# Query weights: ScalarE converts pieces 5, 6 and 7 ahead of the copies of query products 2, 3 and 4

## The chip, the cores and the metric

The kernel runs on one core of a Trainium2 chip. The metric is the device time of one execution in microseconds (us). Before the change, three executions took 1545.81, 1546.57 and 1550.71 us; the median is 1546.57 us.

## The reference, cut to what matters

The program computes three transformer layers over 256 tokens of width 1024, in float32. The change lies in the first layer's feed-forward part, which picks experts by product keys:

```python
def peer_ffn(xn, w_query, subkeys, u_tab, v_tab):
    q = (xt @ w_query).reshape(T, PEER_HEADS, 2, PEER_QDIM // 2)     # 256 tokens, 8 heads x 256
    s = jnp.einsum('thpd,hpkd->thpk', q, subkeys).astype(jnp.float32)
    sv, si = lax.top_k(s, PEER_TOPK)
    # 16 x 16 sums of both halves, top 16 of them: expert ids and softmax gates
    ug = u_tab[ec]
    vg = v_tab[ec]
    act = jax.nn.gelu(jnp.einsum('thkd,td->thk', ug, xc))
    return jnp.einsum('thk,thkd->td', (gc * act), vg)
```

For each of 256 tokens and 8 heads, 16 experts are chosen, and of each of these two rows of 1024 floats are fetched from tables in HBM.

## The kernel before, in words

**Weights in two parts.** Each weight piece (1 MB, 128 x 2048 float32) is loaded by SyncE into a raw buffer. It is then split: ScalarE writes a rounded copy, the high part (`split_hi`, its operation is at line 432), and VectorE or GpSimd subtracts it from the raw data, which gives the low part (`split_lo`, line 439). TensorE multiplies with three passes (high by high, low by high, high by low; lines 2048 to 2050). The high and low parts live in four slots, 0 to 3. `split_hi` waits until the piece that held the slot before has been used by TensorE.

**Query pieces.** The query weights are 8 pieces, one for each head. Pieces 0 to 3 lie in slots 0 to 3, pieces 4 and 6 in slot 2, and pieces 5 and 7 in slot 3. So the high part of piece 4 waits for query product 2, piece 5 for product 3, piece 6 for product 4, and piece 7 for product 5. Query product m is 48 matmuls (`queries(m)`) into one PSUM bank. TensorE's order is: product 1, product 2, the scores of the first heads (`scores(0)`), products 3 to 7, `scores(1)` to `scores(7)` (line 2308), and then the sums of expert rows (line 2332).

**Evacuation in a fixed order.** The semaphore `evac_done` counts the banks that have been emptied, and each copy waits until all earlier jobs were emptied. The order of jobs around the change is written in `PLAN`: query product 2, then the score job of `scores(0)`, then query products 3 to 7, then the other score jobs. ScalarE copies the query products (`query_cols(m)`, line 918). VectorE copies the result of `scores(0)` (line 1660), and it waits for `evac_done` to have counted query product 2.

**VectorE's order** around the change is written out by hand. It does the low part of piece 3, the copy of `scores(0)`, the low parts of pieces 4 and 5, four dot products with expert rows (line 1629), the low parts of pieces 6 and 7, the routing of the second unit, and more dot products:

```python
split_lo(v, "query", 3)
v.wait_ge(evac_done, J["score"])
freed(nc.vector.tensor_copy(SCORE[:, 2 * P:BANK], bank(j)[:, 2 * P:]), j, wait=True)
for n in range(4, 6):
    split_lo(v, "query", n)
```

**Expert rows.** A unit is one head for one half of the tokens, and there are 16 of them. GpSimd issues 16 gathers of 1 MB for each unit (line 627). Their buffers overlay the query weights: gather 6 of the first unit waits for the low part of piece 6, gather 7 for that of piece 7, gathers 9 and 11 for the use of pieces 6 and 7 by TensorE, and gather 13 for all scores. Later units' gathers wait until TensorE has summed the rows that were in the buffers.

Of the kernel before, what the change touches and what calls it, by code (L numbers as in the profile page):

```python
# [80 lines left out]
def query_job(m):  # L81

    return J[f"query_{m}"] if m < 3 else J["query_rest"] + m - 3
# [57 lines left out]
def build(nc, a, out, at):  # L141
    ctx = ExitStack()
    with ctx:
# [44 lines left out]
        PHI = place("ple_hi", [P, 2, S], O_B + 1024, F32R)  # L188
        PLO = place("ple_lo", [P, 2, S], O_B + 1536, F32R)
        C = sb("consts", [P, sum(n for _, n in at.values())])  # L190
        VEC = sb("vec_cols", [P, 72])
        CONV = sb("conv_cols", [P, 2, 4 * 2 * FT])
# [233 lines left out]
        def split_hi(eng, copy, name, n):  # L426

            w = pieces[name, n]
            eng.wait_ge(raw_loaded[w.r], w.landed)
            if w.before is not None:  # L430
                eng.wait_ge(*pieces[w.before].used)
            copy(w.hi[:, :], w.raw[:, :]).then_inc(hi_ready[w.h], 1)  # L432
# [286 lines left out]
        def _(act):  # L719
# [76 lines left out]
            def split(name, n):  # L796
                split_hi(act, act.copy, name, n)
# [112 lines left out]
            def query_cols(m):  # L910
                j = query_job(m)
                act.wait_ge(pe_done, j + 1)
                act.wait_ge(evac_done, j)
                if m == 0:
                    d, src = qT[:, 0:2, P:S], PS[:, j % 8, 2 * P:4 * P]
                else:
                    d, src = qT[:, 2 * m:2 * m + 2, :], PS[:, j % 8, :]
                act.copy(d, src.rearrange("p (c t) -> p c t", c=2)).then_inc(evac_done, 1)
# [6 lines left out]
            def weights(u, q, b):  # L925
                act.wait_ge(sem("dots_done"), u * 4 + (b + 1))
                nc.scalar.activation(r_act[:, b % 2], r_dot[:, b % 2], ACT.Gelu).then_inc(sem("gelu_done"), 1)  # L927
                if b == 0:
                    act.wait_ge(sem("gates_ready"), u + 1)
                act.wait_ge(sem("gelu_done"), u * 4 + (b + 1))  # L930
                for k in range(4):
                    ins = nc.scalar.activation(r_wt[:, b % 2, k:k + 1], r_act[:, b % 2, k:k + 1], ACT.Copy,
                                               scale=r_gate[:, q, 4 * b + k:4 * b + k + 1])
                ins.then_inc(sem("weights_ready"), 1)
# [17 lines left out]
            gate_exp(0)  # L952
            query_cols(1)
            query_cols(0)
            for n in range(4, 8):
                split("query", n)
                query_cols(n - 2)
            weights(0, 0, 0)
            diag(0, 0, wait=False)
            query_cols(6)  # L960
# [225 lines left out]
        def _(v):  # L1186
# [532 lines left out]
            def relative(n):  # L1719

                L, bt, e, _, _ = level(n)
                ref = bt[:, :, L - 1:L].broadcast_to([P, 4 * S // (2 * L), 2 * L])
                step(nc.vector.tensor_tensor(e, bt, ref, ALU.subtract), "h_rel")

            def operands(n):

                L, _, e, qv, kv = level(n)
                if n < 3:
                    v.wait_ge(sem("h_relexp"), 2 * n + 2)
                else:  # L1730
                    v.wait_ge(evac_done, END[f"hg_R{n}"])
                step(nc.vector.tensor_tensor(e[:, :, L:2 * L], e[:, :, L:2 * L], qv[:, :, L:2 * L], ALU.mult), "h_lev", False)
                step(nc.vector.tensor_tensor(e[:, :, 0:L], e[:, :, 0:L], kv[:, :, 0:L], ALU.mult), "h_lev")
# [924 lines left out]
```

## Time and profile before

| quantity | value |
|---|---|
| median of three executions | 1546.57 us |
| profiled execution, own time | 1549.39 us |
| its span on the core | 1547.6 us |
| TensorE busy | 1380.5 us (89%) |
| VectorE busy | 1034.6 us (67%) |
| ScalarE busy | 710.4 us (46%) |
| GpSimd busy | 572.9 us (37%) |
| query products 2 to 7 and scores, in the span | from 170.36 us to about 211.7 us |

Busy time is summed over the whole span, while the stages have different limits. In the rows, PE is TensorE's matmul, PEld its weight load, DVE is VectorE, ACT ScalarE, POOL GpSimd and SP SyncE. `L432` is line 432. A bracket such as `[4.70 <-ACT work_a L918]` says how long the engine was idle just before and what ended that.

### The profile page before, as it was taken

The page shows a single profiled execution, that of the slowest core. Times are in us where ns is not written, and L with a number is a line of the kernel's source. Part 1 is how long each engine was busy: PE and PEld are TensorE (multiplying, and loading weights), DVE is VectorE, ACT ScalarE, POOL GpSimd, SP SyncE. Part 2 cuts the span into 40 slices and gives each one's busy share as a digit, 9 for nine tenths or more (in the row PEclk, how much of TensorE's full clock was granted, in tenths as well). Part 3 has the DMA queues.
Part 4 walks back from the last instruction along what each step waited for, and adds up shares of the span by engine and source line. Part 5 has one row for each costly group of instructions (what it writes and reads, how often), then busy time and mean ns, then how long its engine had stood idle before and what let it go on. Part 6 is the DMA issues. An engine that isn't in the chain of part 4 may idle for free.

```text
span 1547.6 us, 18196 instructions
## 1 busy us (share of the span) xinstructions
PE 1380.5 (89%) x5969; PEld 966.9 (62%) x5969; DVE 1034.6 (67%) x1920; ACT 710.4 (46%) x1377; POOL 572.9 (37%) x537
## 2 busy tenths in 40 slices
PE   7989998778777867877778999999999999999998
PEld 6877973333323323333335879788888778888887
DVE  4896777666666766666655548569863586498733
ACT  5535553223333333223324463477654745776534
POOL 2330454333333333333332421045443612364414
PEclk9999999999999999998998999899999999999999
DMA  9286689999999999999997510557665433476650
GB/s 313 88 144 224 245 353 423 420 422 421 422 421 422 421 422 421 423 421 423 421 420 295 191 33 28 164 163 213 194 215 175 160 140 108 121 207 195 216 192 28
DMA packets 180739, 414.99 MB, mean 268 GB/s; under 512 B 9178, under 2 KB 113218, under 8 KB 148418
## 3 DMA queue, kind: packets, MB, share of 16 engines
q0 software_dynamic: 37440, 268.45, 41.8%
q1 hardware_dynamic: 143090, 145.66, 30.6%
q8 instruction: 38, 0.62, 0.2%
q14 instruction: 27, 0.22, 0.0%
q10 hardware_dynamic: 144, 0.04, 0.0%
HBM read 409.93 MB, written 4.19 MB: 268 GB/s over the span
## 4 chain that ended last, share of the span: by engine, by line
PE 53%; DMA 23%; DVE 9%; ACT 6%; POOL 5%; issue 4%; ACTq 0%; POOLq 0%; DVEq 0%
DMA expert_rows<-in_peer_uv,route_idx 16%; PE ps L2332 10%; PE ps L2501 10%; PE ps L2048 8%; PE ps L2049 8%; PE ps L2050 8%; PE ps L2502 5%; DMA work_b<-in_peer_uv,route_idx 5%; POOL expert_rows L627 2%; DVE weights_lo L439 2%; DMA work_b<-in_peer_u,route_idx 1%; ACT weights_hi L432 1%; POOL weights_lo L587 1%; PE ps L2013 1%; POOL ple_proj_lo L587 1%
## 5 line engine op out<-in xcount | busy, mean ns | idle before, releaser
L1629 DVE CUSTOM_DVE_ANT_0 expert_rows<-expert_rows,ps 128x1024 f32<-128x1024 f32 x180 | 219.4, 1220 | 134.4 <-DMA expert_rows<-in_peer_uv,route_idx 131.5
L2332 PE MATMUL ps<-expert_rows,proj 128*128 128x512 f32 x512 | 244.1, 633 | 65.9 <-ACT proj L941 59.3
L587 POOL TENSOR_TENSOR weights_lo<-weights_raw,weights_hi 128x512 fp32r<-128x512 f32 x120 | 159.7, 1366 | 381.7 <-ACT weights_hi L432 308.5
L627 POOL DMA_INDIRECT expert_rows<-in_peer_uv,route_idx x191 | 184.3, 965 | 285.9 <-PE ps L2332 216.0
L432 ACT CAST weights_hi<-weights_raw 128x2048 fp32r<-128x2048 f32 x98 | 185.4, 1917 | 101.8 <-PE ps L2050 81.6
L2332 PEld LDWEIGHTS ps<-expert_rows,proj 128*128 128x128 f32 x512 | 100.9, 202 | 208.2 <-issue 127.5
L2501 PE MATMUL ps<-x_normT,weights_hi 128*128 128x512 f32 x640 | 222.5, 394 | 0.0
L439 DVE TENSOR_TENSOR weights_lo<-weights_raw,weights_hi 128x2048 fp32r<-128x2048 f32 x68 | 160.6, 2370 | 64.1 <-ACT weights_hi L432 63.7
L927 ACT ACTIVATE proj<-proj 128x4 f32<-128x4 f32 x64 | 13.1, 205 | 411.7 <-DVE proj L1629 404.6
L2048 PE MATMUL ps<-weights_hi,x_normT 128*128 128x512 f32 (+1 forms) x496 | 189.6, 382 | 12.7 <-DVE weights_lo L439 7.4
L2049 PE MATMUL ps<-weights_lo,x_normT 128*128 128x512 f32 (+1 forms) x496 | 185.8, 375 | 0.0
L2050 PE MATMUL ps<-weights_hi,x_normT 128*128 128x512 f32 (+1 forms) x496 | 185.7, 374 | 0.0
L2502 PE MATMUL ps<-x_normT,weights_lo 128*128 128x256 f32 x640 | 177.3, 277 | 0.0
L2332 PE MATMUL ps<-expert_rows,scratch 128*128 128x512 f32 x252 | 121.7, 630 | 28.2 <-ACT scratch L941 28.2
L2501 PEld LDWEIGHTS ps<-x_normT,weights_hi 128*128 128x128 f32 x640 | 120.0, 188 | 27.9
L2502 PEld LDWEIGHTS ps<-x_normT,weights_lo 128*128 128x128 f32 x640 | 120.2, 188 | 0.0
L2048 PEld LDWEIGHTS ps<-weights_hi,x_normT 128*128 128x128 f32 x496 | 94.2, 190 | 34.6 <-issue 8.0
L2332 PEld LDWEIGHTS ps<-expert_rows,scratch 128*128 128x128 f32 x252 | 49.8, 202 | 99.0 <-issue 59.5
L2050 PEld LDWEIGHTS ps<-weights_hi,x_normT 128*128 128x128 f32 x496 | 94.1, 190 | 16.9
L2049 PEld LDWEIGHTS ps<-weights_lo,x_normT 128*128 128x128 f32 x496 | 94.3, 190 | 15.8 <-issue 0.2
L1860 DVE SCALAR_TENSOR_TENSOR work_a<-ps,conv_cols,work_a 128x254 f32<-128x254 f32 (+1 forms) x176 | 76.4, 475 | 29.3 <-ACT work_a L1076 25.2
L694 POOL TENSOR_TENSOR hidden_hi<-work_a 128x256 f32 (+1 forms) x44 | 41.9, 951 | 100.3 <-ACT work_a L1056 100.0
(367 smaller groups left out, 2413.2 us busy)
## 6 DMA issues: line engine op xcount, KB each, us to landing
weights_raw<-in_ffn_up SPq DMA_DIRECT2D x88, 512.0 KB, 5.1
weights_raw<-in_ffn_down SPq DMA_DIRECT2D x22, 1024.0 KB, 4.9
weights_raw<-in_ab_w_in SPq DMA_DIRECT2D x14, 1024.0 KB, 5.2
weights_raw<-in_w_in SPq DMA_DIRECT2D x12, 1024.0 KB, 7.9
weights_raw<-in_ple_gate SPq DMA_DIRECT2D x8, 1024.0 KB, 6.6
weights_raw<-in_c_w_in SPq DMA_DIRECT2D x6, 1024.0 KB, 5.9
weights_raw<-in_w_out SPq DMA_DIRECT2D x4, 1024.0 KB, 12.4
weights_raw<-in_peer_w_query SPq DMA_DIRECT2D x4, 1024.0 KB, 12.2
```

Of the source, the lines that this page charges most:

```text
L432: copy(w.hi[:, :], w.raw[:, :]).then_inc(hi_ready[w.h], 1)
L439: eng.tensor_tensor(w.lo[:, :], w.raw[:, :], w.hi[:, :].bitcast(F32), ALU.subtract).then_inc(lo_ready[w.h], 1)
L587: ins = pool.tensor_tensor(w.lo[:, c], w.raw[:, c], w.hi[:, c].bitcast(F32), ALU.subtract)
L627: nc.gpsimd.indirect_dma_start(out=dst, out_offset=None, in_=table, in_offset=bass.IndirectOffsetOnAxis(ap=r_idx[:, q, n:n + 1], axis=0)). ...
L1629: ins = nc.vector.tensor_tensor_reduce(out=rows, in0=rows, in1=tokens, scale=1.0, scalar=0.0, op0=ALU.mult, op1=ALU.add, accum_out=r_dot[: ...
L1860: ins = nc.vector.scalar_tensor_tensor(out=d, in0=PS[:, (j0 + 2 * q + g) % 8, 0:S - n], scalar=CONV[:, l, bass.ds(i * RING + (tap * 2 * FT ...
L2048: pe.matmul(o, x[0], w[0], start=first, stop=False)
L2049: pe.matmul(o, x[0], w[1], start=False, stop=False)
L2050: return pe.matmul(o, x[1], w[0], start=False, stop=last)
L2332: ins = pe.matmul(PS[:, (J[f"peer_{t}"] + m) % 8, :], DIAG[b][:, k, :], rows[:, m * BANK:(m + 1) * BANK], start=False, stop=False, skip_gr ...
L2501: pe.matmul(b.rearrange("p (a t) -> p a t", a=2), hi[:, c, g, :], x_both(c), start=c == 0, stop=False)
L2502: ins = pe.matmul(b[:, 0:S], lo[:, c, g, :], XHI[:, c, :], start=False, stop=c == KC - 1)
```

## The change

ScalarE's order in the query stage is changed. Before, it converted piece n and then copied product n - 2, for n from 4 to 7. After it, piece 4 is converted first, then pieces 5, 6 and 7 are each converted ahead of the copy of products 2, 3 and 4, and the copy of product 5 follows at the end. The same instructions are issued, with the same waits.

```diff
             gate_exp(0)
             query_cols(1)
             query_cols(0)
-            for n in range(4, 8):
+            split("query", 4)
+            for n in range(5, 8):
                 split("query", n)
-                query_cols(n - 2)
+                query_cols(n - 3)
+            query_cols(5)
             weights(0, 0, 0)
             diag(0, 0, wait=False)
             query_cols(6)
```

| ScalarE's order | before | after |
|---|---|---|
| 1 | convert 4 | convert 4 |
| 2 | copy 2 | convert 5 |
| 3 | convert 5 | copy 2 |
| 4 | copy 3 | convert 6 |
| 5 | convert 6 | copy 3 |
| 6 | copy 4 | convert 7 |
| 7 | convert 7 | copy 4 |
| 8 | copy 5 | copy 5 |

## Rows read from the trace of the kernel before

**Rows 1.** The page: DMA share and GB/s in 40 slices; the last chain's shares.

```profile
DMA  9286689999999999999997510557665433476650
GB/s 313 88 144 224 245 353 423 420 422 421 422 421 422 421 422 421 423 421 423 421 420 295 191 33 28 164 163 213 194 215 175 160 140 108 121 207 195 216 192 28
DMA expert_rows<-in_peer_uv,route_idx 16%; PE ps L2332 10%; PE ps L2501 10%; PE ps L2048 8%; PE ps L2049 8%; PE ps L2050 8%; PE ps L2502 5%; DMA work_b<-in_peer_uv,route_idx 5%; POOL expert_rows L627 2%; DVE weights_lo L439 2%; DMA work_b<-in_peer_u,route_idx 1%; ACT weights_hi L432 1%; POOL weights_lo L587 1%; PE ps L2013 1%; POOL ple_proj_lo L587 1%
```

**Rows 2.** Windows, 190 to 210: length, each engine's busy time, PEclk, DMA share, GB/s.

```profile
190.00:195.00 5.00, 5.00 (x44) 5.00 (x44) 3.73 (x5) 1.63 (x3) 0.50 (x1) 1.00 0.60 249
195.00:200.00 5.00, 5.00 (x44) 5.00 (x43) 3.76 (x10) 4.85 (x12) 1.21 (x2) 1.00 0.62 213
200.00:205.00 5.00, 5.00 (x44) 5.00 (x43) 4.72 (x22) 2.30 (x5) 3.01 (x4) 1.00 0.80 287
205.00:210.00 5.00, 5.00 (x46) 5.00 (x46) 4.90 (x10) 2.93 (x5) 2.89 (x2) 1.00 1.01 395
```

**Rows 3.** Chain of waits, 140 to 420: start, length, what.

```profile
205.60 6.25 PE ps L2308 x56
...
256.51 19.62 DMA expert_rows<-in_peer_uv,route_idx
```

**Rows 4.** Timeline of ScalarE: start, length, instruction, idle before.

```profile
176.45 1.91 ACT L432 CAST weights_hi<-proj 128x2048 fp32r<-128x2048 f32 x1 [4.98 <-PE ps L2050]
178.26 0.58 ACT L918 COPY work_a<-ps 128x512 f32<-128x512 f32 x1
182.65 1.90 ACT L432 CAST weights_hi<-scratch 128x2048 fp32r<-128x2048 f32 x1 [3.81 <-PE ps L2050]
184.46 0.58 ACT L918 COPY work_a<-ps 128x512 f32<-128x512 f32 x1
188.41 1.91 ACT L432 CAST weights_hi<-expert_rows 128x2048 fp32r<-128x2048 f32 x1 [3.38 <-PE ps L2050]
...
194.17 1.90 ACT L432 CAST weights_hi<-expert_rows 128x2048 fp32r<-128x2048 f32 x1 [3.37 <-PE ps L2050]
```

**Rows 5.** Timeline of VectorE.

```profile
151.99 2.29 DVE L439 TENSOR_TENSOR weights_lo<-weights_raw,weights_hi 128x2048 fp32r<-128x2048 f32 x1 [0.65 <-ACT weights_hi L432]
...
178.87 0.42 DVE L1660 COPY proj<-ps 128x256 f32<-128x256 f32 x1 [4.70 <-ACT work_a L918]
179.32 2.29 DVE L439 TENSOR_TENSOR weights_lo<-proj,weights_hi 128x2048 fp32r<-128x2048 f32 x1
184.65 2.29 DVE L439 TENSOR_TENSOR weights_lo<-scratch,weights_hi 128x2048 fp32r<-128x2048 f32 x1 [3.04 <-ACT weights_hi L432]
...
191.44 2.28 DVE L439 TENSOR_TENSOR weights_lo<-expert_rows,weights_hi 128x2048 fp32r<-128x2048 f32 x1
196.17 2.29 DVE L439 TENSOR_TENSOR weights_lo<-expert_rows,weights_hi 128x2048 fp32r<-128x2048 f32 x1 [2.44 <-ACT weights_hi L432]
```

**Rows 6.** Timeline of TensorE: the first matmuls of a product after a wait, and of products 3 and 4.

```profile
154.34 0.38 PE L2048 MATMUL ps<-weights_hi,x_normT 128*128 128x256 f32 x1
...
176.56 0.36 PE L2048 MATMUL ps<-x_normT,weights_hi 128*128 128x256 f32 x1
...
182.39 0.28 PE L2048 MATMUL ps<-x_normT,weights_hi 128*128 128x256 f32 x1
```

**Rows 7.** Timeline of GpSimd: gathers 6 and 7 of the first unit.

```profile
194.50 0.94 POOL L627 DMA_INDIRECT expert_rows<-in_peer_uv,route_idx  x1 [14.55 <-DVE weights_lo L439]
199.24 0.94 POOL L627 DMA_INDIRECT expert_rows<-in_peer_uv,route_idx  x1 [3.79 <-DVE weights_lo L439]
```

**Rows 8.** TensorE after its two longest later idles: timeline rows.

```profile
831.65 0.77 PE L2048 MATMUL ps<-weights_hi,x_normT 128*128 128x512 f32 x1 [2.74 <-DVE weights_lo L439]
...
839.65 1.97 PE L2013 MATMUL ps<-consts,x_res 128*128 128x128 f32 x8 [3.65 <-DVE x_res L1308]
```

**Rows 9.** Windows of one us after those two restarts.

```profile
834.00:835.00 1.00, 1.00 (x5) 0.83 (x4) 0.96 (x2) 0.00 (x0) 0.00 (x0) 0.70 1.06 406
...
844.00:845.00 1.00, 1.00 (x4) 0.81 (x3) 0.40 (x2) 0.91 (x5) 0.00 (x0) 0.57 0.02 8
```

## The prediction

> **What bounds the kernel now.** I began with the page's slices and its chain. The reader sees a long middle stretch in which the DMA engines are saturated at about 421 GB/s, which are the gathers of expert rows, and a chain that spends 16% of the span on those gathers [rows 1]. The question is what decides when that stretch begins. The windows around it answer: between 190 and 205 us the DMA engines are busy for 0.60, 0.62 and 0.80 of the time, and only from 205 us on for all of it, while TensorE is busy for the whole of each 5 us [rows 2]. The chain of waits says the same: it runs through TensorE up to the scores (56 matmuls at 205.60 us) and first passes through a gather at 256.51 us [rows 3]. So in the query stage TensorE sets the time, and the gathers behind it are started by what TensorE and the splitting of weights release.
>
> Then I read the three engines' timelines side by side. TensorE goes straight from product 3 (176.56) into product 4 (182.39): 5.83 us for one product, no idle time [rows 6]. ScalarE waits for TensorE ahead of every conversion: 4.98, 3.81, 3.38 and 3.37 us, and always on the product whose slot it overwrites [rows 4]. VectorE waits 4.70 us for the copy of product 2 before it may copy the scores (178.87), and only behind that comes the low part of piece 4, from 179.32 to 181.61 [rows 5]. TensorE needs that low part at 182.39. Its cover is 182.39 - 181.61 = 0.78 us, and that is all the slack there is.
>
> **The change part by part.** Nothing is added or removed: no instruction, no DMA, no semaphore. Five copies and conversions trade places, and what matters is which waits they now stand behind.
>
> *Conversions 5, 6 and 7 earlier by one copy: gain nothing.* Each starts when its product has ended. Conversion 5 starts at 182.65, 0.26 us after product 4 started, and ScalarE had been idle for 3.81 us before it [rows 4]. The copy that stood ahead of it was long done. From below the gain is 0, and from above it is at most one copy, 0.58 us, if a conversion had ever waited for one; the idle times exclude that, so I take 0.
>
> *Copy of product 2, behind conversion 5: this is the cost.* Conversion 5 waits for product 3, which TensorE ends at about 182.4 in either kernel. The conversion then runs from 182.65 and the copy behind it starts at 184.46, as the copy of product 3 did, and ends at 184.46 + 0.58 = 185.04 [rows 4]. VectorE's copy of the scores starts 0.03 us after that copy (178.87 against 178.26 + 0.58), so now at 185.07. The low part of piece 4 follows after 0.45 us (179.32 - 178.87), at 185.52, and ends at 185.52 + 2.29 = 187.81 [rows 5]. Handing a low part to TensorE costs 0.06 us (154.34 against 151.99 + 2.29) [rows 5, 6]. Product 4 therefore starts at 187.87 instead of 182.39: TensorE stands still for 5.48 us. The first matmul after a wait holds TensorE for a little longer than one in a row (0.36 to 0.28), which adds 0.08. Term: 5.5 us.
>
> What is queued behind the waiting copy on ScalarE is only conversion 6, and that waits for product 4 anyway. Behind VectorE's waiting copy stand the low parts of pieces 4 and 5; TensorE waits for the first, and the second is done at 187.81 + 2.29 = 190.1, well ahead of product 5 (187.87 + 5.83 = 193.7). SyncE's loads of pieces 6 and 7 wait for product 1 and don't move. GpSimd's queue stays as it is.
>
> *Clock after the stall.* TensorE has nowhere in this stretch stood still for so long; the nearest rows are two restarts after idles of 2.74 and 3.65 us [rows 8]. After the first the granted clock is at the lower level (1.2 GHz of 2.4) until about 834.6: the window 834 to 835 has a mean of 0.70, so 0.6 of it was at half [rows 9]. That is 834.6 - 831.65 = 2.95 us. After the second it is low until 844.86 (mean 0.57: 0.86 at half), 5.2 us. At half clock half of that time is lost: 1.5 and 2.6 us. An idle of 5.5 us is longer than both, so a fall is to be expected; I take the middle, 2.0 us, as an estimate. Its ends are 0 (no fall) and 2.6, and a little more for a longer low stretch, 3.3.
>
> The Trainium skill, page "TensorE: Matmul & The Clock Gate", Part 1, says of modelling that "the ramp penalty is <1% of a typical kernel span" and that one should not fit a count of cold matmuls. By that advice the term would be left out, and the sum would be the stall alone (the first rival below). The two restarts in rows 8 and 9 speak against leaving it out here, where it is a quarter of the effect.
>
> *Is there a second stall?* With the clock's term product 5 starts at 187.87 + 5.83 + 2.0 = 195.7 and product 6 at 201.4. Conversion 6 starts 0.26 after product 5's start, 196.0, ends at 197.9, and its low part is done at 200.2, 1.2 us before product 6. VectorE's four dots (4.5 us, the time between the end of the low part of piece 5, 186.94, and the start of that of piece 6, 191.44) are done by then, at 194.6. Piece 7 goes the same way, 5.7 us later. The copies of products 3, 4 and 5 have nobody waiting for them before the scores at the end. So no second stall: 0.
>
> *What the delay becomes.* Gather 6 was released by the low part of piece 6 (191.44 + 2.28 = 193.72, issued at 194.50) and gather 7 by that of piece 7 (198.46, issued at 199.24) [rows 5, 7]. Both low parts follow TensorE, by about 6.5 and 7.5 us later. Gathers 9, 11 and 13 wait for products 6 and 7 and for the scores. The DMA engines were partly idle between 190 and 205 [rows 2], so there is no stock of issued gathers with which to use the extra time. Their saturated stretch starts about 7.5 us later, and as the same 1 MB gathers then flow at the same rate [rows 1], it ends 7.5 us later. The layers behind it depend on its result, so nothing gives it back.
>
> **Sum.** 5.5 + 2.0 = 7.5 us. Against the profiled execution's own time (span 1547.6, time 1549.39) that is 1556.9. That execution is 2.8 us above the median of the three shown, so against the median it is 1546.57 + 7.5 = 1554.1 us, and that is what I forecast (1.005 of before).
>
> **Rivals.**
>
> *The clock stays up.* The stall alone would be 5.5 us: 1552.1. For it: the rows have only two restarts, with low stretches as different as 2.95 and 5.2 us, so the length is not a constant of the kernel. Against: both were behind idles shorter than this one, and both had a low stretch.
>
> *The gathers swallow the delay (not slower).* If the saturated stretch were limited by a backlog that exists before gather 7, starting TensorE's part 7.5 us later would cost nothing. It decides from the point at which gathers already issued would keep the DMA engines busy until the delayed ones come, some 7 us of work at 200 us. For it: the stretch from 205 us on is DMA-bound. Against: 0.60 and 0.62 busy in the two windows before; the unused 5 x (0.40 + 0.38 + 0.20) = 4.9 us show that there is no backlog there. Price 0: 1546.6; half swallowed gives 1550.3.
>
> *VectorE takes the ready low part ahead of the waiting copy (not slower).* Then the stall vanishes: 1546.6. In the trace the high part of piece 4 was ready at 178.36, VectorE idle, and yet the low part started only behind the copy, at 179.32 [rows 4, 5]. So it goes in order. The Trainium skill, page "Perfetto Trace Analysis", section "Per-engine timelines", calls ScalarE's, VectorE's and GpSimd's execution "strict FIFO"; the trace agrees.
>
> *A second stall at piece 6 or 7.* Their slack is 1.2 us; if a slowed TensorE or a late dot used it up, 1 to 3 us come on top: up to 1557.
>
> **How the numbers follow.** The forecast (stall and a fall of the clock, all of it passed on) gets 0.70, the stall alone 0.10, a second stall 0.05, delay half or wholly swallowed 0.12, in order or other surprises on the fast side 0.03. What a measurement of this kernel can tell from no change is about 0.3%, 4.6 us, so "same" reaches from 1541.9 to 1551.2. The forecast, the stall alone and the second stall lie above that; since executions of before alone spread over 4.9 us, I leave 0.02 of them to "same". Slower 0.83, same 0.14, faster 0.03. The range goes from 1550.3 (half swallowed) to 1557.4 (clock term 3.3 and a small second wait or spread of the executions).
>
> **What would show it right or wrong.** After the change VectorE's line 1660 should wait about 10.9 us instead of 4.7 (it is free from 174.2) and start at 185.1; TensorE should show one idle of about 5.3 us before a matmul of line 2048 at 187.9, released by the low part of line 439, and a granted clock under 1 in the 5 us behind it; gather 7 should be issued at about 206.7 and `scores` begin at about 213. The DMA share in 195 to 205 us should fall well under 0.6. If TensorE has no idle there, the argument is wrong at its root; if it has and the end does not move, the swallowing rival was right.

## The result and the profile after

Twelve executions of the changed kernel have a median of 1554.62 us, twelve of the kernel before 1547.28 us. The ratio is 1.0051 with a 95% interval of 1.0041 to 1.0062: slower by 7.3 us in the medians, 7.9 us by the ratio (6.3 to 9.6 us by its interval). The forecast was 1554.1 us and 1.005.

The profiled execution after has its own time of 1553.87 us (span 1552.1). In the changed file every line behind the edit is two higher: 1660 became 1662, and 2048 to 2050 became 2050 to 2052. The traces also begin at slightly different points: conversion 4 starts at 176.45 before and at 176.55 after, so 0.10 us is to be taken off every shift of the second trace.

ScalarE's timeline after (start, length, instruction, idle before), which answers to [rows 4]:

```profile
176.55 1.91 ACT L432 CAST weights_hi<-proj 128x2048 fp32r<-128x2048 f32 x1 [4.98 <-PE ps L2052]
182.75 1.90 ACT L432 CAST weights_hi<-scratch 128x2048 fp32r<-128x2048 f32 x1 [4.29 <-PE ps L2052]
184.55 0.58 ACT L918 COPY work_a<-ps 128x512 f32<-128x512 f32 x1
196.20 1.91 ACT L432 CAST weights_hi<-expert_rows 128x2048 fp32r<-128x2048 f32 x1 [11.07 <-PE ps L2052]
198.01 0.57 ACT L918 COPY work_a<-ps 128x512 f32<-128x512 f32 x1
201.96 1.91 ACT L432 CAST weights_hi<-expert_rows 128x2048 fp32r<-128x2048 f32 x1 [3.37 <-PE ps L2052]
```

Conversion 5 starts when it did before, since it waits for the same product. The copy of product 2 is now at 184.55 instead of 178.26. VectorE's timeline after, to [rows 5]:

```profile
185.16 0.42 DVE L1662 COPY proj<-ps 128x256 f32<-128x256 f32 x1 [10.90 <-ACT work_a L918]
185.62 2.29 DVE L439 TENSOR_TENSOR weights_lo<-proj,weights_hi 128x2048 fp32r<-128x2048 f32 x1
187.83 2.28 DVE L439 TENSOR_TENSOR weights_lo<-scratch,weights_hi 128x2048 fp32r<-128x2048 f32 x1
...
198.21 2.29 DVE L439 TENSOR_TENSOR weights_lo<-expert_rows,weights_hi 128x2048 fp32r<-128x2048 f32 x1 [3.52 <-ACT weights_hi L432]
203.97 2.29 DVE L439 TENSOR_TENSOR weights_lo<-expert_rows,weights_hi 128x2048 fp32r<-128x2048 f32 x1 [3.47 <-ACT weights_hi L432]
```

The copy of the scores waited 10.90 us instead of 4.70, and the low part of piece 4 ends at 187.91. TensorE's timeline after, to [rows 6], and its granted clock (the column ahead of the last two) in windows of one us:

```profile
187.96 0.58 PE L2050 MATMUL ps<-x_normT,weights_hi 128*128 128x256 f32 x1 [5.31 <-DVE weights_lo L439]
188.34 0.41 PE L2051 MATMUL ps<-x_normT,weights_hi 128*128 128x256 f32 x1
```

```profile
185.00:186.00 1.00, 0.00 (x0) 0.00 (x0) 0.80 (x2) 0.13 (x1) 0.00 (x0) 0.99 1.04 417
186.00:187.00 1.00, 0.00 (x0) 0.00 (x0) 1.00 (x1) 0.00 (x0) 0.00 (x0) 0.50 1.00 418
...
192.00:193.00 1.00, 1.00 (x7) 1.00 (x7) 1.00 (x3) 0.00 (x0) 0.00 (x0) 0.59 0.91 369
193.00:194.00 1.00, 1.00 (x10) 1.00 (x10) 1.00 (x3) 0.00 (x0) 0.00 (x0) 1.00 0.16 66
```

Product 4 starts 5.47 us late (187.96 - 182.39 - 0.10). The clock fell to half during the idle and came back at about 192.8 (the mean of 0.59 means 0.82 us at half): 4.9 us of product 4 ran at half clock. What that cost is seen at the scores. They begin at 213.23 in TensorE's timeline, against 205.43 before: 7.70 us later with the offset taken off, of which 5.47 are the stall and 2.23 the clock and the restart.

GpSimd's gathers 6 and 7, to [rows 7], and the DMA share (the last column but one) in windows of 5 us, to [rows 2]:

```profile
201.28 0.94 POOL L627 DMA_INDIRECT expert_rows<-in_peer_uv,route_idx  x1 [21.24 <-DVE weights_lo L439]
207.04 0.94 POOL L627 DMA_INDIRECT expert_rows<-in_peer_uv,route_idx  x1 [4.82 <-DVE weights_lo L439]
```

```profile
190.00:195.00 5.00, 5.00 (x34) 5.00 (x33) 4.69 (x9) 0.00 (x0) 0.00 (x0) 0.72 0.63 257
195.00:200.00 5.00, 5.00 (x44) 5.00 (x43) 1.79 (x1) 2.39 (x2) 0.00 (x0) 1.00 0.00 0
200.00:205.00 5.00, 5.00 (x44) 5.00 (x43) 1.53 (x2) 2.95 (x3) 0.94 (x1) 1.00 0.40 120
205.00:210.00 5.00, 5.00 (x44) 5.00 (x44) 4.83 (x20) 4.83 (x13) 2.35 (x3) 1.00 0.52 164
```

The DMA engines stand still from 195 to 200 us, where before they were busy for 0.62 of the time. There was nothing to move.

**Where the profiled pair differs from the medians.** The two profiled spans are only 4.5 us apart. Followed through the trace, the shift is still 7.4 us where TensorE waits at 965.65 before and at 973.10 after (7.45 less the offset), and 4.5 at the next such wait, 987.18 and 991.76. Between them the profiled execution of before ran at a lower clock, and the one after did not. The windows of before:

```profile
970.00:975.00 5.00, 5.00 (x24) 3.07 (x22) 3.50 (x4) 1.65 (x3) 0.00 (x0) 0.61 1.05 397
975.00:980.00 5.00, 5.00 (x25) 3.58 (x22) 3.20 (x4) 0.59 (x1) 0.00 (x0) 0.50 1.19 297
980.00:985.00 5.00, 5.00 (x23) 4.28 (x23) 4.82 (x7) 4.49 (x4) 0.00 (x0) 0.86 0.45 113
```

After, the windows from 975 to 990 have 1.00. Of the thirteen traces of this study four show such a fall here, those of before and of runs 1, 4 and 10, with and without the stall in the query stage, so it does not belong to the change. In that pair it masked 2.9 us of the 7.4, and the executions' medians are the better measure.

### The profile page after: what moved, and what is told of

The parts are those of the page before. It is cut to its first block, busy times and chain, and to the rows that moved or that the text cites. A ratio compares the mean times of both kernels' runs of the same rounds, so it can differ in the third digit from the quotient of the medians.

```text
span 1552.1 us, 18196 instructions
## 1 busy us (share of the span) xinstructions
PE 1378.4 (89%) x5969; PEld 965.9 (62%) x5969; DVE 1034.7 (67%) x1920; ACT 710.4 (46%) x1377; POOL 570.3 (37%) x537
## 4 chain that ended last, share of the span: by engine, by line
PE 51%; DMA 23%; DVE 10%; ACT 6%; issue 5%; POOL 5%; ACTq 0%; POOLq 0%; DVEq 0%; SPq 0%
DMA expert_rows<-in_peer_uv,route_idx 15%; PE ps L2503 10%; PE ps L2050 8%; PE ps L2334 8%; PE ps L2052 8%; PE ps L2051 8%; DMA work_b<-in_peer_uv,route_idx 7%; PE ps L2504 5%; DVE weights_lo L439 2%; POOL expert_rows L627 2%; ACT weights_hi L432 2%; POOL weights_lo L587 1%; DMA weights_raw<-in_ab_w_in 1%; PE ps L2015 1%; POOL ple_proj_lo L587 1%
## 5 line engine op out<-in xcount | busy, mean ns | idle before, releaser
L2051 PEld LDWEIGHTS ps<-weights_lo,x_normT 128*128 128x128 f32 x496 | 94.3, 190 | 15.8 <-issue 0.2
```

Source lines behind the costliest of these rows:

```text
L2051: pe.matmul(o, x[0], w[1], start=False, stop=False)
```

## The experiments

A ratio is that of a kernel's time to the time of before, measured beside it, with its 95% interval; 0.1% is 1.55 us. Where starts in two traces are compared with the offset taken off, the offset is again read from conversion 4 (176.45 us in the kernel before).

### 1 and 2: which of the moved copies does it

Experiment 1 moves only the copy of product 2:

```diff
-            for n in range(4, 8):
-                split("query", n)
-                query_cols(n - 2)
+            split("query", 4)
+            split("query", 5)
+            query_cols(2)
+            query_cols(3)
+            for n in range(6, 8):
+                split("query", n)
+                query_cols(n - 2)
```

> Only the copy of query product 2 goes behind conversion 5; conversions 6 and 7 keep their places. Chain theory (copy 2 releases VectorE's copy of the scores, that the low part of piece 4, that TensorE's product 4): the whole effect is here, one TensorE idle of 5.3 us at 182.5 to 187.9, half clock for some 5 us, 7 to 8 us slower than before (ratio 1.005), the same as the full change. Rival (the three earlier conversions share the effect, or the gathers' release): a third of it, 2 to 3 us.

Measured: 1.0037 (1.0024 to 1.0051), 5.7 us, somewhat less than the 7 to 8 us expected. TensorE has the same idle:

```profile
188.55 0.58 PE L2052 MATMUL ps<-x_normT,weights_hi 128*128 128x256 f32 x1 [5.31 <-DVE weights_lo L439]
```

Experiment 2 moves everything else:

```diff
-            for n in range(4, 8):
-                split("query", n)
-                query_cols(n - 2)
+            split("query", 4)
+            query_cols(2)
+            split("query", 5)
+            for n in range(6, 8):
+                split("query", n)
+                query_cols(n - 3)
+            query_cols(5)
```

> Copy 2 keeps its place; only conversions 6 and 7 go ahead of the copies of products 3 and 4. Chain theory: no TensorE idle, no change (ratio 1.000, within 0.15%). Rival (every move costs something): 1.002 to 1.004.

Measured: 1.0000 (0.9989 to 1.0010). There is no wait of TensorE for a low part in this stage. The two together say that the cost sits in the copy of product 2 alone, and that conversions 6 and 7 gain nothing by going first. The ratio of the first is lower than the full change's 1.0051, but the intervals overlap, and the traces agree: with the offsets taken off, the scores begin 7.70 us later than before in run 1 as in the full change, and 0.04 us later in run 2.

### 3: the link through VectorE

The full change, with VectorE's low part of piece 4 ahead of its copy of the scores:

```diff
             split_lo(v, "query", 3)
+            split_lo(v, "query", 4)
             j = J["score"]
             v.wait_ge(evac_done, j)
             freed(nc.vector.tensor_copy(SCORE[:, 2 * P:BANK], bank(j)[:, 2 * P:]), j, wait=True)
-            for n in range(4, 6):
-                split_lo(v, "query", n)
+            split_lo(v, "query", 5)
```

> The full change, and VectorE does the low part of piece 4 ahead of its copy of the first scores, so that this copy no longer stands in front of it. Chain theory: TensorE's idle is gone although copy 2 is as late as in the full change, and the time is that of before (ratio 1.000, within 0.15%). If the order on ScalarE alone did it: 1.005 stays.

Measured: 1.0003 (0.9991 to 1.0014). VectorE's timeline of this kernel, and the one wait that TensorE is left with:

```profile
178.38 2.29 DVE L439 TENSOR_TENSOR weights_lo<-proj,weights_hi 128x2048 fp32r<-128x2048 f32 x1 [4.31 <-ACT weights_hi L432]
184.98 0.42 DVE L1663 COPY proj<-ps 128x256 f32<-128x256 f32 x1 [4.32 <-ACT work_a L918]
185.44 2.29 DVE L439 TENSOR_TENSOR weights_lo<-scratch,weights_hi 128x2048 fp32r<-128x2048 f32 x1
```

```profile
194.57 0.38 PE L2050 MATMUL ps<-x_normT,weights_hi 128*128 128x256 f32 x1 [0.58 <-DVE weights_lo L439]
```

ScalarE's order is that of the full change and the copy of the scores is just as late (184.98), but nothing that TensorE needs at once waits for it, and the loss is gone from the time. The remaining 0.58 us is the low part of piece 6, pushed back because that of piece 5 now stands behind the late copy; the scores begin 0.8 us later than before. So it was not ScalarE's order in itself, but the low part queued behind the waiting copy on VectorE.

### 4 and 8: the clock's part

Dummy matmuls (ahead of product 4) keep TensorE busy during the wait, in the full change. First 24 of them:

```diff
             for m in range(3, 8):
+                if m == 4:
+                    spin(query_job(4), 24)
                 queries(m)
```

> The full change, with 24 dummy matmuls (128 x 256, about 0.216 us each, 5.2 us in all) ahead of product 4, so that TensorE is busy while it waits for the low part. Stall plus clock theory: the 5.4 us stay, the granted clock stays at 1.00, the 2.4 us of the clock's fall are saved: 5.4 us slower than before (ratio 1.0035), scores begin at about 211.1 instead of 213.4. Rival (the clock's fall costs nothing on the path): the same time as the full change, 1.005.

Measured: 1.0057 (1.0044 to 1.0070). I had mis-sized the dummy: in float32 each one shows as two matmul records, and 24 took 10.5 us, twice what I had written. TensorE was held until 192.8, 4.9 us beyond the end of the low part, so this run could not decide. With 12:

> The full change with 12 dummy matmuls ahead of product 4. The run with 24 showed 0.43 us for one, so 12 take 5.2 us and end just before the low part of piece 4 does (187.9). Stall plus clock theory: no idle over 0.5 us, granted clock 1.00, scores begin at about 211.2 us of the span, 5.6 us slower than before (1.0036), 2.2 us faster than the full change. If the clock's fall cost nothing: 1.005 and scores at 213.4.

Measured: 1.0028 (1.0016 to 1.0039). TensorE's timeline:

```profile
182.66 5.35 PE L2009 MATMUL ps<-consts 128*128 128x256 f32 x24
188.13 0.39 PE L2050 MATMUL ps<-x_normT,weights_hi 128*128 128x256 f32 x1
...
211.27 6.42 PE L2310 MATMUL ps<-work_b,work_a 128*128 128x128 f32 x56
```

The granted clock stays at 1.00 through 180 to 195 us. With the offsets taken off (0.26 us here, 0.10 in the full change), product 4 starts at 187.87 in this run and at 187.86 in the full change, but the scores begin at 211.01 instead of 213.13. The fall of the clock thus has its own price, 2.1 us at the scores. In the time of the whole kernel that price is less sharp. The interval of the full change (from 1.0041) does not touch this one, and the two ratios differ by 3.6 us; but run 1, with the same idle and the same fall, has 1.0037, which is 1.4 us above this run with overlapping intervals. The 2.1 us lie between the two differences, and neither measures them.

### 5, 6 and 9: is a pure delay passed on

The same dummy matmuls in the kernel before, with nothing else changed: 24 (run 5), 60 (run 6) and 12 (run 9).

> The kernel before, with 24 dummy matmuls ahead of product 4: a pure delay of TensorE by 5.2 us with no order changed and no idle time. If a delay in the query stage is passed on in full: 5.2 us slower (ratio 1.0034). If the DMA-bound gathers swallow it: 1.000 to 1.001.

> The kernel before, with 60 dummy matmuls ahead of product 4: 13 us of delay. Passed on in full: 1.0084 and a slope of 1 between this run and the one with 24. Swallowing theory with a stock of gathers of some 5 us: only the part above it, about 8 us (1.005).

> The kernel before with the same 12 dummy matmuls: TensorE delayed by 5.2 us and nothing else changed. Passed on in full: scores begin at about 210.8, 5.1 us slower than before (1.0033), half of what 24 cost. If the change had a second cost beside TensorE's delay (in the gathers' order, say), the run above would be slower than this one by more than 0.5 us.

| dummies | their time | scores later by | last sum later by | ratio | interval | in us |
|---|---|---|---|---|---|---|
| 12 | 5.35 | 5.2 | 4.9 | 1.0027 | 1.0014 to 1.0039 | 4.2 |
| 24 | 10.53 | 10.4 | 9.5 | 1.0064 | 1.0039 to 1.0089 | 9.9 |
| 60 | 26.07 | 25.9 | 25.2 | 1.0158 | 1.0132 to 1.0185 | 24.5 |

(The second to fourth columns are read from the traces, in us, with the offsets taken off; the last sum of expert rows ends the first layer's part, at 828.30 us before.)

The first two expectations carry the wrong length of a dummy (0.216 us instead of 0.43). With the right one, all three fit a slope of about one: the time grows by 24.5 - 4.2 = 20.3 us from 12 dummies to 60, the start of the scores by 20.7 us. For the first 5 us the time alone is weak evidence, since its interval reaches from 2.2 to 6.0 us; in the trace the last sum moves by 4.9 of 5.2 us.

The traces also say where the delay is handed on. The first gather of the second unit is released by TensorE's sums for the first, and it is issued 15.8 us behind the start of the scores before, after and in all three of these runs. From that gather to the last sum it takes 605 to 608 us in every trace of this study, and between 225 and 825 us the DMA engines move 420 to 422 GB/s in all thirteen. So nothing in between gives the delay back.

Runs 8 and 9 have the same ratio, one with the order of the change and one with that of before, and so nearly have runs 4 and 5 (1.0057 and 1.0064, scores 10.4 us later in both). The reordering thus has no second cost of more than some 2 us beside TensorE's delay; the 0.5 us of my expectation is finer than these runs can tell.

### 7, 10 and 11: in the other direction

If a delay of TensorE costs its length, is an advance worth as much? Run 7 fills the DMA engines' idle time: gather 8, whose buffer is free at 187 us, goes ahead of gathers 6 and 7, in the kernel before.

```diff
-                for n in range(TOPK):
+                for n in (0, 1, 2, 3, 4, 5, 8, 6, 7, *range(9, TOPK)):
```

> The kernel before, with gather 8 of the first unit (whose buffer is free as soon as piece 5 is split, at about 187 us) issued ahead of gathers 6 and 7, so that 1 MB (2.5 us) moves while the DMA engines are partly idle. If the start of the saturated stretch is set by the bytes still to be moved: 2.5 us faster (0.9984). If it is set by TensorE's release of the buffers at 221 us, at which the queue has just run dry: no change (within 0.5 us).

Measured: 0.9997 (0.9983 to 1.0012). No change is the better fit, but the 2.5 us lie just inside the interval. Run 10 takes 1.9 us of TensorE away ahead of the first sums:

```diff
-                for acc in accs:
+                for acc in accs if t else ():
                     pe.matmul(acc, zeros, C[:, 0:BANK], start=True, stop=False, skip_group_check=True)
...
-    rows[:, m * BANK:(m + 1) * BANK], start=False,
+    rows[:, m * BANK:(m + 1) * BANK], start=first and n == 0,
```

> The kernel before, without the two matmuls that fill the accumulators of the first eight units with zeros ahead of their first sum (1.9 us at 211.7); the first matmul of each accumulator starts it in their place. The result is the same sum. If each us of TensorE ahead of the first release of row buffers is worth one us in this direction as well: release at about 219.5 instead of 221.2, 1.7 us faster than before (0.9989). If the gathers' bytes bind from here on: no change, and a DMA queue that does not run dry at 223 to 225 us.

Measured: 0.9997 (0.9986 to 1.0008). The gain of 1.7 us did not show, but the interval holds its ratio of 0.9989 as well as 1.000, so the time decides between neither. The timelines show what moved. The last dot of the first unit on VectorE and TensorE's first sum of the second unit, in the kernel before:

```profile
226.06 1.23 DVE L1629 CUSTOM_DVE_ANT_0 work_b<-work_b,x_norm 128x1024 f32<-128x1024 f32 x1 [1.24 <-DMA work_b<-in_peer_uv,route_idx]
```

```profile
243.15 15.70 PE L2332 MATMUL ps<-expert_rows,proj 128*128 128x512 f32 x32 [2.11 <-issue]
```

in run 7:

```profile
224.91 1.23 DVE L1629 CUSTOM_DVE_ANT_0 work_b<-work_b,x_norm 128x1024 f32<-128x1024 f32 x1 [1.16 <-DMA work_b<-in_peer_uv,route_idx]
```

```profile
242.00 7.13 PE L2332 MATMUL ps<-expert_rows,proj 128*128 128x512 f32 x16 [0.92 <-ACT proj L941]
```

and in run 10, whose trace begins 1.4 us later than that of before:

```profile
245.20 15.71 PE ps L2332 x32
```

```profile
228.17 1.23 DVE L1629 CUSTOM_DVE_ANT_0 work_b<-work_b,x_norm 128x1024 f32<-128x1024 f32 x1 [1.25 <-DMA work_b<-in_peer_uv,route_idx]
```

(The first of these two is from the chain of waits, the second from the timeline.) Run 7 moved VectorE's last dot 1.15 us forward, but GpSimd's first gather for the second unit waited for TensorE's release as before (221.25 against 221.21). Run 10 moved that release 1.7 us forward (220.89 against 221.21 + 1.4), but VectorE's last dot came 0.7 us later (228.17 against 226.06 + 1.4), and so did the second unit's first sum. My reading was that two paths run side by side here, the landings with VectorE's dots and TensorE's release of buffers, that they meet at the second unit, and that each edit shortened only one.

Run 11 has both:

> The two edits that gained nothing alone, together in the kernel before: gather 8 ahead of 6 and 7, and no zero fill. Two-path theory (the first one moved VectorE's dots and ScalarE's weights 1.15 us earlier while TensorE's release stayed; the second moved the release 1.7 us earlier while the landings stayed): together both come earlier, TensorE starts the second unit's sums 1.1 to 1.7 us earlier than in the kernel before, and the time falls by 1.1 to 1.7 us (0.9990). If the bytes of the gathers alone bind by now: no change (1.000).

Measured: 0.9990 (0.9975 to 1.0006), medians 1545.88 and 1547.75. Its timelines of TensorE and GpSimd:

```profile
241.70 14.00 PE L2332 MATMUL ps<-expert_rows,proj 128*128 128x512 f32 x32 [2.33 <-ACT proj L941]
...
826.44 0.61 PE L2350 MATMUL ps<-consts 128*128 128x128 f32 x4
```

```profile
219.54 1.88 POOL L627 DMA_INDIRECT expert_rows<-in_peer_uv,route_idx  x1 [2.92 <-PE ps L2332]
```

The second unit's sums start 1.45 us earlier than before and the last sum is at 826.44 instead of 828.30. The trace moves as expected, and the ratio is the expected one; but its interval includes 1, so a gain in time is not shown. Nor is the reading with two paths. One trace of each kernel is too little for shifts of this size: in run 2, whose edit moves no release and whose ratio is 1.0000, the last sum comes 1.5 us earlier than before (826.34, the trace being 0.44 us ahead) although the second unit's sums start 1.0 us later. Whether an advance is worth as much as a delay stays open.

## Why the prediction was right

- **The stall.** Forecast: product 4 at 187.87, VectorE's line 1660 waiting 10.9 us. Measured: 187.96 and 10.90 us. The sum of waits and durations from neighbouring rows was right to 0.1 us. Run 1 shows that the late copy of product 2 is enough for the stall, and run 3, which takes the low part out from behind VectorE's copy, removes it.
- **Conversions first gain nothing.** Run 2: 1.0000, and conversion 6 starts when it did before (187.97, and 188.41 less 0.44).
- **The clock.** Forecast 2.0 us with ends 0 and 3.3; measured 2.23 with the restart, for a low stretch of 4.9 us after it. The term was taken between two rows that differed by a factor of nearly two, so its closeness is partly luck. That it fell at all after this idle is what the traces of the full change and of run 1 show; the prediction's grounds for it were thin (see below the list). The figure that the Trainium skill's page "TensorE: Matmul & The Clock Gate" (Part 1) gives, under 1% of the span, holds: 2.1 us are 0.14% of it. But leaving the term out would have missed more than a quarter of the 7.7 us at the scores, as run 8 shows.
- **No second stall.** TensorE has no further idle before the scores. Low parts of pieces 6 and 7 end at 200.5 and 206.26.
- **Passed on in full.** The total was right, and runs 5, 6 and 9 speak against the swallowing rival, by time and by trace. My picture of it was too simple, though. I had the saturated stretch begin with gather 7 and end later by the same amount, as if bytes alone counted from 205 us on. In the kernel before the queue of gathers nearly runs dry at 224 to 225 us (262 GB/s in that window against 410 to 434 around it), which points to the release of the second unit's buffers at 221.21, 15.8 us behind the scores, as its start. Gather 7 and that release both hang on products 4 to 7, so the simple sum came out.
- **The order on VectorE.** The rival in which it takes the ready low part first would have shown no idle; it had 5.31 us.

**What the clock's term rested on.** The two restarts in [rows 8] are not the ones behind the two longest later idles. In the kernel before TensorE has 35 idles of 2.7 to 3.5 us between 262 and 800 us. Behind 16 of them the granted clock fell to half, and behind 19 it stayed at 1.00, the longest of these 3.40 us (before 549.78). One that it stayed up behind, with a window that follows:

```profile
280.01 7.13 PE L2332 MATMUL ps<-expert_rows,proj 128*128 128x512 f32 x16 [2.96 <-ACT proj L941]
```

```profile
284.00:285.00 1.00, 1.00 (x4) 0.52 (x3) 0.98 (x3) 0.00 (x0) 0.00 (x0) 1.00 1.07 434
```

The rival in which the clock stays up thus had more for it than the prediction said, which knew only two idles, both with a low stretch. What spoke against it is that this idle was to be longer than any of those 35. Only the wait for the first data at the start of the program, 8.08 us, is longer in that trace, and behind it the profile shows 1.00 as well.

## What to carry to other kernels

Before an instruction is moved behind one that waits, follow who waits for it over every engine in turn: here an early conversion on ScalarE held back a copy, that a copy on VectorE, and that the weights TensorE needed, which had only 0.78 us to spare. The conversions themselves could not start earlier, since each waited for TensorE's use of its slot. An idle of TensorE can cost more than its length, as a fall of the clock may come on top: here 5.5 us became 7.7. And a stage whose end releases the work of a saturated queue passed on its delays in full, for lengths from 5 to 26 us; that an advance is worth as much does not follow, and these runs do not show it.

## What the runs showed of the hardware

A dummy float32 matmul of 128 x 256 takes 0.43 us of TensorE (12 of them 5.35 us, as 24 records), against 0.12 us for one in the split format fp32r. With TensorE filled by such matmuls for 5.35 us the granted clock stayed at 1.00, while with 5.31 us of idle time it was at half for 4.9 us behind it.
